# HGRN projections of a two-layer decoder step: seven of eight tile pairs instead of six through the seven-product scheme, with the moves that make room for it

## What is computed

```python
q, f_logit, i, z = jnp.split(x @ w_in, 4, axis=-1)      # 2048 -> 4 x 2048
f = lb + (1.0 - lb) * jax.nn.sigmoid(f_logit)
k = (1.0 - lb) * jax.nn.sigmoid(-f_logit)
q = jax.nn.silu(q) * HGRN_DK ** -0.5
# per head of 128 channels, chunkwise, exact per token:
#   S <- diag(f) S + k v^T,   o = q S
o = o * lax.rsqrt(jnp.mean(o * o, axis=-1, keepdims=True) + NORM_EPS) * norm_w
out = (o * jax.nn.silu(z)) @ w_o
```

## Time and profile before

| what | value |
|---|---|
| median of 3 timed runs | 2843.78 us (2841.17 to 2852.16) |
| profiled execution, its own time | 2853.62 us |
| span of the profiled execution | 2851.8 us |
| TensorE busy | 2730.1 us (96%), 36816 matmuls |
| VectorE busy | 1608.9 us (56%) |
| ScalarE busy | 1259.1 us (44%) |
| GpSimd busy | 138.4 us (5%) |

### The profile page before, as it was taken

How to read it: one execution, slowest core, us unless ns; L and a number is a source line. 1 busy time by engine, 2 the same in 40 slices (tenths; PEclk the granted TensorE clock), 3 DMA queues, 4 the chain that set the end, 5 groups by cost and what they waited for, 6 DMA issues and landing times. The chain is left out here.

```text
span 2851.8 us, 82517 instructions
## 1 busy us (share of the span) xinstructions
PE 2730.1 (96%) x36816; PEld 2567.6 (90%) x36816; DVE 1608.9 (56%) x2679; ACT 1259.1 (44%) x1869; POOL 138.4 (5%) x116
## 2 busy tenths in 40 slices
PE   6999999999999999999889988999999999999997
PEld 5899999999998887888779978999999999999997
DVE  7335313313326777888742267776777767775224
ACT  5345323324414555555532255444544455444222
POOL 0000000000001111010000003000000000000000
PEclk8999999999999999999999999999999999999999
DMA  3333333333311111112132242222333223243322
GB/s 126 108 106 113 109 113 113 113 111 134 115 69 52 50 53 54 51 53 71 43 111 89 90 155 73 95 95 94 97 100 107 95 80 114 95 139 137 124 89 102
DMA packets 86816, 273.48 MB, mean 96 GB/s; under 512 B 16448, under 2 KB 29504, under 8 KB 65984
## 3 DMA queue, kind: packets, MB, share of 16 engines
q1 hardware_dynamic: 77248, 250.37, 26.5%
q10 hardware_dynamic: 9216, 17.83, 1.7%
HBM read 221.63 MB, written 46.54 MB: 94 GB/s over the span
## 5 line engine op out<-in xcount | busy, mean ns | idle before, releaser
L136 PE MATMUL w_pair<-a_x_hi,keep_w_hi 128*128 128x272 f32 x2016 | 428.4, 294 | 19.3 <-DVE a_x_lo L1059 18.5
L136 PE MATMUL w_pair<-a_x_lo,keep_w_hi 128*128 128x272 f32 x2016 | 419.7, 289 | 0.0
L136 PE MATMUL w_pair<-a_x_hi,keep_w_lo 128*128 128x272 f32 x2016 | 417.4, 288 | 0.0
L1045 DVE TENSOR_TENSOR keep_w_lo<-keep_raw,keep_w_hi 128x2048 fp32r<-128x2048 f32 x63 | 144.4, 2293 | 469.5 <-ACT keep_w_hi L798 469.5
L136 PEld LDWEIGHTS w_pair<-a_x_hi,keep_w_hi 128*128 128x128 f32 x2016 | 320.2, 189 | 25.7 <-issue 20.7
L136 PEld LDWEIGHTS w_pair<-a_x_lo,keep_w_hi 128*128 128x128 f32 x2016 | 318.1, 189 | 0.0
L136 PEld LDWEIGHTS w_pair<-a_x_hi,keep_w_lo 128*128 128x128 f32 x2016 | 317.8, 189 | 0.0
L136 PE MATMUL t_pair<-t_x_hi,keep_w_hi 128*128 128x272 f32 x1216 | 262.0, 297 | 18.2 <-DVE t_x_lo L2421 9.1
L136 PE MATMUL t_pair<-t_x_lo,keep_w_hi 128*128 128x272 f32 x1216 | 253.5, 290 | 0.0
L136 PE MATMUL t_pair<-t_x_hi,keep_w_lo 128*128 128x272 f32 x1216 | 253.3, 290 | 0.0
L812 ACT ACTIVATE a_stage<-w_pair 128x544 f32<-128x544 f32 x64 | 40.0, 625 | 425.1 <-PE w_pair L136 425.1
(11 more groups left out here) (448 smaller groups left out, 6146.7 us busy)
## 6 DMA issues: line engine op xcount, KB each, us to landing
keep_raw<-in_w_in SPq DMA_DIRECT2D x64, 1024.0 KB, 5.0
keep_raw<-in_hgrn_in SPq DMA_DIRECT2D x64, 1024.0 KB, 5.1
keep_raw<-in_rwkv_wo SPq DMA_DIRECT2D x16, 1024.0 KB, 5.0
keep_raw<-in_hgrn_wo SPq DMA_DIRECT2D x16, 1024.0 KB, 5.0
t_Ss<-in_hgrn_s SPq DMA_DIRECT2D x16, 512.0 KB, 7.1
out_hgrn_s<-t_Sd SPq DMA_DIRECT2D x16, 512.0 KB, 8.5
scr_r<-a_stage ACTq DMA_DIRECT2D x16, 272.0 KB, 2.2
scr_k<-a_stage ACTq DMA_DIRECT2D x16, 272.0 KB, 2.1
```

The lines of the kernel that those rows point to most:

```text
L136: mm = pe.matmul(out[:, a, 0:TH], w, x[:, kt, a * TH:(a + 1) * TH], start=(kt == order[0] and n == 0), stop=(kt == order[-1] and n == 2))
L1045: dve.tensor_tensor(w_lo[b][:, :], raw[n % 2][:, :], w_hi[b][:, :].bitcast(F32), ALU.subtract).then_inc(p.raw_lo, 1)
```

## The change

`U` goes from 6 to 7: seven pairs of row tiles (14 of 16) go through the products, an item is 896 columns wide instead of 768, the remainder is two row tiles, 256 columns instead of 512, and a pair has 49 + 8 = 57 sub-steps. A pair now takes 147 + 24 matmuls.

To make room in memory, S1 is written over its own source in raw tile 1, so the third sum, which reads that source, must come before it; the order is third, first, second sum everywhere, and the last item slot of all shares the place of S2 and S3. A seventh combination of rows is made in head 0's tail.

The rest is order: in the gates pair the state chain stands ahead of the fourth sum and item 3, ScalarE copies the turned keys ahead of item 2, and the steps of the head before are put behind sub-steps 3, 9 and 18 to 33. In the values pair the third sum stands ahead of the first, the first query product behind the second sum, and the second and third level behind 16 and 25. TensorE waits for the combined rows ahead of product 2 instead of product 0 in the first pair.

```diff
-U = 6
+U = 7
@@ memory
-        S1 = sb("wS1", [P, UW])
+        S1 = raw[1][:, 0:UW]
@@ seven_products
                 if q == 0:
                     pe.wait_ge(s.evac, GS - 1)
-                    pe.wait_ge(s.t_lo, 2 * U)
...
                 pe.wait_ge(s.p1, q + 1)
+                if q == 0:
+                    pe.wait_ge(s.t_lo, 2 * U)
                 product(2, X, False)
@@ TensorE's steps
-                    steps = dict(zip((13, 16, 18, 20, 22, 24, 27, 30), late(e - 1)))
+                    steps = dict(zip((18, 20, 22, 24, 26, 28, 30, 33), late(e - 1)))
                     if e > 1:
-                        steps.update(zip((3, 8), keys))
+                        steps.update(zip((3, 9), keys))
                     seven_products(2 * e - 2, steps)
-                    steps = {m: L(i) for i, m in enumerate((11, 14, 24, 31, 37, 42, 47, 51))}
+                    steps = {m: L(i) for i, m in enumerate((11, 16, 25, 31, 37, 42, 47, 51))}
@@ ScalarE
             def gates_pair(e, q):
+                if e > 1:
+                    k_copy(e - 1)
                 item_hi(q, 2)
                 if e > 1:
                     act.wait_ge(s.evac, H0 + 4 * e)
                     act.wait_ge(s.q1s, q)
                     silu(zs, s.zs)
-                    k_copy(e - 1)
...
                 if e == 0:
                     sums_hi(4)
                     sums_hi(5)
+                    scaled_rows(6)
...
                 k_copy(e)
                 if e < KT - 1:
-                    for j in range(U):
+                    for j in range(U - 1):
                         third_sum_hi(j)
+                    sums_hi(U - 1)
+                    third_sum_hi(U - 1)
@@ VectorE
+                dve.tensor_tensor(S3[:, :], raw[0][:, 0:UW], S1, ALU.subtract).then_inc(s.s3, 1)
+            def weight_sum_1(q):
+                dve.wait_ge(s.s3, q + 1)
+                dve.tensor_tensor(S1, S1, raw[1][:, UW:2 * UW], ALU.add).then_inc(s.s1, 1)
@@ VectorE, gates_pair
-                weight_sum_3(q)
                 item_lo(q, 2)
+                if e > 1:
+                    chain(e - 1)
                 weight_sum_4(q)
                 item_lo(q, 3)
-                if e > 1:
-                    chain(e - 1)
                 item_lo(q, 4)
@@ VectorE, values_pair
                 lower_first(q - 1, qr)
+                weight_sum_3(q)
                 weight_sum_1(q)
+                weight_sum_2(q)
                 first_q(e)
-                weight_sum_2(q)
                 item_lo(q, 2)
                 item_lo(q, 3)
                 take(e, 0)
                 widen(e, 0)
-                weight_sum_3(q)
                 weight_sum_4(q)
...
                 lower_second(q, zs)
                 if q < NQ - 1:
+                    weight_sum_3(q + 1)
                     weight_sum_1(q + 1)
                     weight_sum_2(q + 1)
@@ VectorE, tail of head 0
                 if e == 0:
                     rest_lo(0, 0)
-                    weight_sum_1(0)
...
-                    for j in range(U):
+                    for j in range(U - 1):
                         third_sum_lo(j)
+                    sums_lo(U - 1)
+                    third_sum_lo(U - 1)
                     chain(e)
                     scaled_out(n + 3, zs)
+                    weight_sum_3(0)
+                    weight_sum_1(0)
                     weight_sum_2(0)
```

42 lines of the change are left out of this document (23 added, 19 removed).

## The result

The changed kernel takes 2867.44 us (median of 4 runs, 2864.70 to 2873.88), the kernel before 2846.94 us in the same comparison (4 runs). The ratio is 1.0073, 95% interval 1.0054 to 1.0092: slower by 15 to 26 us. The forecast was 2863 us and slower.

A forecast was written before the change was run, and what follows sets the result against it. TensorE was taken as the bound, with VectorE right beside it in the values pairs. Head 1's +8.0 us and 13 x 0.85 = +11.0 made +19 on the 2843.78 us median: 2863 us, range 2838 to 2875.

The forecast's parts named there:

- VectorE's stretch: VectorE's nearly unbroken work from the gates pair's item 6 to the values pair's third widening; would end 1.53 us later.
- TensorE gets 0.38 us a pair: Each of 28 pairs: three matmuls fewer, 0.38 us a pair, 10.5 us in all.
- The sums of squares come later: Gates pair: moved from sub-step 30 to 33, 1.13 us later less 0.2 of the state products, +0.93 us.
- The contention: Values pair: GpSimd's scaling stops the remainder's subtraction (2.24 us), so shortening it saves only its own 0.27 us.
- The third rival, a shared rate: Remainder's subtraction beside GpSimd runs slower rather than stopped, shrinking to 1.36 us; -9 us, 2854 us; chance 0.20.
- A head: Each of heads 2 to 14: 1.23 us later at the level, less 0.38 after it, +0.85 us.
- stops of about 1 us at product 1: Sign in the values pairs: TensorE waits some 1 us at product 1 for item 1's low part.
- 0.4 to 0.6 at the level behind 37: Sign in the values pairs: TensorE waits 0.4 to 0.6 us for VectorE at the level after sub-step 37.
- The first pair: Start: 1.4 us delay before it, 5.6 us stop at product 2, less 0.38; second pair starts 6.6 us later.
- the unfavourable case: First pair: GpSimd's operations fall upon VectorE's preparation of item 2, making its low part ready 2.4 us later than 1761.0.
- The cover holds: Rival: VectorE's stretch isn't late, so TensorE's 10.5 + 2.6 us are gained; 2838 us with the start's cost; chance 0.17.
- More stops: Rival: VectorE's lateness survives the gates pair or stops restart TensorE's pipeline; 1 us a head, +14, 2877 us; chance 0.13.

The follow-up runs named there:

- e2: Changed kernel with only the sums of squares moved, from behind sub-step 33 to 36; 2874.2 us, ratio 1.0089 to the kernel before.
- e3: Kernel before with only the sums of squares moved, from behind sub-step 30 to 33; 2857.2 us, ratio 1.0031 to the kernel before.
- e1: Changed kernel with a head's late steps four sub-steps earlier, sums of squares behind 29; 2844.7 us, ratio 0.9984 to the kernel before.
- e4: Changed kernel with GpSimd clearing the sample states' buffer instead of scaling the states into it; 2864.2 us, ratio 1.0052 to the kernel before.
- e6: Changed kernel with late steps earlier, sums of squares behind 28, four sub-steps after the sample states' products; 2842.4 us, ratio 0.9980 to the kernel before.
- e7: Changed kernel with the state chain put back behind item 3, as it stood before; 2871.2 us, ratio 1.0076 to the kernel before.
- e8: Changed kernel with the values pair's second level behind sub-step 14 instead of 16; 2872.7 us, ratio 1.0083 to the kernel before.
- e10: Kernel before with late steps moved, sums of squares behind 28, four sub-steps after the sample states' products; 2840.6 us, ratio 0.9975 to the kernel before.
- e5: Changed kernel, head 0's tail only: first pair's three sums right behind the sixth row combination, item 2 before the state chain; 2862.8 us, ratio 1.0044.
- e9: Changed kernel with the edits of e6 and e5 together; 2833.7 us, ratio 0.9947 to the kernel before.

## Why the forecast was right, and where its terms were off

It forecast +19 us: 8.0 in head 1 and 11.0 in the 13 others. Measured by the rows: +1.6 before the first pair (below), +7.0 in it, and +8.5 in the other 27, together +17.1, beside +20.5 between the medians (15 to 26). The sign, the cause and the place were right. The terms that were mis-sized are the lateness of VectorE's stretch (1.53 forecast, 1.20 measured), which made the heads' part 11.0 instead of 7.3, and the first pair with its lower clock, which my sum did not have (6.6 forecast at the start, 8.6 measured). One was too large and the other too small, so a part of the closeness is two errors that offset each other.

**TensorE gets 0.38 us a pair.** Right: behind the level at sub-step 37 the values pair takes 29.12 - 18.15 = 10.97 us instead of 27.86 - 16.52 = 11.34. The gates pair went from 30.44 to 29.75, forecast 29.9: the 0.38 and the wait for the turned keys (0.2 forecast) are gone, and no row of TensorE's weight loads for the keys is left after the first pair; the other 0.1 has no row.

**The sums of squares come later.** Forecast +0.93 us from the pair's start; measured 2244.25 - 2224.56 = 19.69 against 2231.25 - 2212.40 = 18.85: +0.84. That this starts the stretch late, and costs a head 0.75 us for three sub-steps, is what e2 and e3 show; e1 shows that an earlier place heals it.

**The stretch.** From the gates pair's start, item 1's low part ends at 33.34 (2257.90) instead of 32.26: +1.08, forecast 1.16. From the first of the sums to item 2's low part it is 4.35 us (2258.17 to 2262.52) instead of 3.35: +1.00, forecast 1.10. The dependent sums follow each other at 1.12 us (2258.17, 2259.29, 2260.42), not at 1.18: the extra 0.18 us for a dependence, which I took from sums of 768 columns between other work, was 0.12 too much over the two. The third widening ends at 47.80 (2272.36) instead of 46.60: +1.20, forecast 1.53.

**The contention.** Here the picture was wrong in place. I carried 2.24 - 0.27 us for the remainder's subtraction under GpSimd's scaling. The remainder now took 0.40 us, and the hold fell on an operation behind it, the third widening's 1.82 us instead of 0.41. Why it moved is not shown: the remainder's subtraction starts 0.20 us after GpSimd's scaling in both kernels (2255.80 and 2255.60, 2269.57 and 2269.37). But the scaling takes 2.37 us instead of 1.90 in every head, 0.47 more, as if GpSimd were now the one held first; no run tests it. The pair of both costs 0.40 + 1.82 = 2.22 instead of 2.24 + 0.41 = 2.65: -0.43, where I had -0.27, and this is half of the 0.33 us by which the stretch's end was off. e4 shows that all of it is worth no more than 0.17 us a head, because product 2 stops TensorE first. The third rival, a shared rate, falls with the 1.82 us, where it would give 1.33, and with the 0.40.

**A head** thus costs 1.63 - 0.69 - 0.38 = +0.56 us instead of +0.85; times 13 it is 7.3 instead of 11.0. In the same terms I had 1.81 - 0.58 - 0.38: the stops were too large by 0.18, and the gates pair gave 0.11 more than I said. The forecast sign "stops of about 1 us at product 1" stands (0.94); the one "0.4 to 0.6 at the level behind 37" was off: 1.63 - 1.44 = 0.19.

**The first pair.** The wait for the turned keys grew from 1.45 to 2.73 us, and from the state products' start to product 0 it is 1.21 (1746.76 to 1747.97) instead of 0.91, the clock being low from about 1747.4 on: +1.6, forecast 1.4. Item 2's low part was ready at 1761.32, forecast 1761.0, but by two errors that offset each other: VectorE reached the state chain at 1752.33, 2.8 us later than before and not 3.9, and GpSimd's scaling fell upon the second sum (2.67 instead of 1.09 us), which I had as the unfavourable case. The stop was 4.56 us, at the low end of 4.2 to 6.6. The term that was missing is the clock: the pair is 7.0 us longer, and 7.0 + 0.38 - 4.56 = 2.8 us of it are no stop. Inside the pair TensorE worked at 1.2 GHz from 1747.97 to 1750.7 and for 2.93 us after the stop, 5.7 us, which at half speed is 2.8 us at most. So the second pair starts 1.6 + 7.0 = 8.6 us later than before, not 6.6.

**The rivals.** "The cover holds" is what e1 and e6 made true: it forecast 2838 us with the start's cost and they take 2844.7 and 2842.4, with first pairs that the clock made longer than the 7 us of that sum. It decided where I said it would, by the time at which VectorE's stretch starts, and lost by less than my count said. "More stops" did not come: the gates pairs after the first are at 29.75 us and without a row of waits; the hidden wait for the additions stood there before, too.

**What stays open.** Why the lower clock lasted 3.4 us after the stop of the changed kernel and 13.7 us after a shorter one in e6 is not explained by any row here (the table at the end). The order of the instructions alone is not it: the first pair is in the same order in the changed kernel, e7 and e8, and it lasted 3.4, 6.8 and 3.4 us there, and 20.5 in e4, where only GpSimd's scaling is another. Nor do the rows say where the other 3.4 us of the medians' difference lie, nor why the first pair starts up to 12 us apart between executions.

## What to carry to other kernels

When an edit makes the bounding engine faster, look for the engine that feeds it in the busiest stage and count its chain from the wait that starts it: here one step of a hand-written order, three sub-steps too late, took back about what six matmuls a head gave (0.75 and 0.76 us). Read the starts on both sides of each hand-over, and not only the view of waits: a wait of some 0.37 us, repeated 14 times, stood in no row of it and was worth as much as half of the seventh product. And a stop in a prologue can be dearer than it is long, so cut it before the steady state is judged by the total: e6 and e10 differ by 0.8 us a head in favour of e6, and their totals (2842.4 and 2840.6) do not show it.

## What the runs showed of the hardware

Around the first pair TensorE's granted clock went to its lower level (0.50 to 0.56 in the rows, 1.2 GHz) and back as follows; read in steps of 0.5 us from the profiled execution of each, us:

| kernel | wait for the keys | low after it | wait inside the pair | low after it |
|---|---|---|---|---|
| before | 1.45 | none | none | none |
| after | 2.73 | 3.4 | 4.56 | 3.4 |
| e1 | 2.73 | 3.4 | 2.84 | 13.7 |
| e2 | 2.74 | 3.4 | 4.61 | 3.4 |
| e4 | 2.27 | none | 3.75 | 20.5 |
| e5 | 2.72 | 3.4 | 2.34 | 3.4 |
| e6 | 2.73 | 3.4 | 2.35 | 13.7 |
| e7 | 2.27 | none | 5.32 | 6.8 |
| e8 | 2.73 | 3.4 | 4.61 | 3.4 |
| e9 | 2.7 | 3.4 | 1.35 | none |

How long it stayed low does not follow the length of the wait, and in e6 TensorE was busy for 13.63 of 14 us of it. The Trainium skill (TensorE: Matmul & The Clock Gate, Part 1: The HAM clock gate) tells that the array falls back to 1.2 GHz after it was idle, and these rows agree with that much.

An operation of VectorE with two inputs in SBUF and 256 columns took 1.82 us beside GpSimd's scaling and 0.41 without it, while another of the same size, started 0.20 us into the same scaling, took 0.40 us. So not every operation that overlaps is held, and when the one that used to be hit (2.24 us with 512 columns) was shortened, the hit fell on a later one.
